# A chunk scan whose keys are turned by a product with a diagonal of decays, and whose state is advanced in PSUM

## The reference

```
def step(s, inp):
    r_t, w_t, k_t, v_t, kk_t, a_t = inp
    sa = einsum('bhvk,bhk->bhv', s, kk_t)
    s = s * w_t - sa (kk_t * a_t)^T + v_t k_t^T
    return s, einsum('bhvk,bhk->bhv', s, r_t)
```

## Time and profile before

| | us |
|---|---|
| three runs | 2038.17, 2038.21, 2041.07 |
| median | 2038.21 |
| profiled execution, its own time | 2040.22 |
| its span in the profile | 2038.6 |
| PE busy | 1709.5 (84%) |
| DVE busy | 1323.0 (65%) |
| ACT busy | 631.4 (31%) |
| POOL busy | 1162.7 (57%) |

### The profile page before, as it was taken

One profiled execution on the slowest core, in us unless ns is written; L12 is line 12 of the kernel. 1 busy time (PEld: TensorE's weight loads), 2 busy tenths in 40 slices (PEclk: granted clock), 3 DMA queues, 4 the chain that ended last, 5 costly groups with the idle time before them and its releaser, 6 DMA issues.

```text
span 2038.6 us, 25920 instructions
## 1 busy us (share of the span) xinstructions
PE 1709.5 (84%) x8602; PEld 827.1 (41%) x8602; DVE 1323.0 (65%) x3428; ACT 631.4 (31%) x1490; POOL 1162.7 (57%) x1555
## 2 busy tenths in 40 slices
PE   7999999889878999899989777777777777777776
PEld 2544435777765644444444222222222222222222
DVE  1278873577765886566666667666676666766653
ACT  3245532356543432322222222222222222222221
POOL 2100012565543767766667777776777776777773
PEclk9999999999999999999999999999999999999999
DMA  7356645445456999999999999999999999999996
GB/s 259 97 191 231 213 133 169 127 126 126 120 185 215 380 379 407 405 405 405 405 406 409 409 409 409 409 409 401 409 409 409 409 409 376 408 410 409 409 410 238
DMA packets 282158, 659.72 MB, mean 324 GB/s; under 512 B 71248, under 2 KB 120496, under 8 KB 282032
## 3 DMA queue, kind: packets, MB, share of 16 engines
q0 software_dynamic: 150336, 552.67, 68.4%
q1 hardware_dynamic: 131696, 105.46, 17.2%
HBM read 635.49 MB, written 22.54 MB: 323 GB/s over the span
## 4 chain that ended last, share of the span: by engine, by line
DMA 34%; PE 19%; POOL 9%; issue 4%; DVE 3%; ACT 1%; SPq 0%; POOLq 0%; ACTq 0%; DVEq 0%
DMA arena<-in_peer_v_dram,arena 28%; PE banks L2006 10%; POOL arena L1607 9%; DMA arena<-in_peer_u_dram,arena 5%; PE banks L2027 4%; PE banks L557 3%; DVE arena L1946 2%; PE banks L1508 1%; DMA arena<-in_w_out_dram 1%; PE banks L2077 0%; PE banks L2035 0%; POOL arena L1642 0%; DVE arena L1918 0%; PE banks L1516 0%; DVE arena L1844 0%
## 5 line engine op out<-in xcount | busy, mean ns | idle before, releaser
L2006 PE MATMUL banks<-arena 128*128 128x512 f32 x1984 | 948.6, 608 | 247.3 <-DMA arena<-in_peer_v_dram,arena 228.7
L1946 DVE CUSTOM_DVE_ANT_0 arena<-arena,banks 128x1024 f32<-128x1024 f32 x512 | 623.3, 1220 | 398.5 <-DMA arena<-in_peer_u_dram,arena 398.4
L2006 PEld LDWEIGHTS banks<-arena 128*128 128x128 f32 x1984 | 347.6, 190 | 836.3 <-issue 466.0
L1607 POOL DMA_INDIRECT arena<-in_peer_v_dram,arena x504 | 472.1, 937 | 218.1 <-PE banks L2006 114.3
L1607 POOL DMA_INDIRECT arena<-in_peer_u_dram,arena x512 | 481.8, 941 | 185.8 <-issue 130.5
L1660 ACT ACTIVATE arena<-arena 128x128 f32<-128x128 f32 x496 | 190.3, 400 | 695.3 <-PE banks L2006 694.5
L1135 PE MATMUL banks<-arena 64*64 64x64 f32 (+1 forms) x2688 | 109.1, 232 | 14.1 <-POOL arena L789 6.3
L2617 PE MATMUL banks<-arena 128*128 128x512 f32 x224 | 111.8, 606 | 0.7 <-ACT arena L2275 0.7
L1135 PEld LDWEIGHTS banks<-arena 64*64 64x64 f32 x2688 | 96.5, 138 | 29.0 <-issue 12.8
L2713 PE MATMUL banks<-arena 128*128 128x512 f32 x192 | 86.9, 609 | 1.2 <-issue 1.2
L2027 PE MATMUL banks<-arena 128*128 128x384 f32 x256 | 85.5, 485 | 0.8 <-ACT arena L1370 0.8
(11 more groups left out here) (325 smaller groups left out, 2023.3 us busy)
## 6 DMA issues: line engine op xcount, KB each, us to landing
arena<-in_w_mod_dram SPq DMA_DIRECT2D x18, 1024.0 KB, 7.2
arena<-in_peer_wq_dram SPq DMA_DIRECT2D x16, 1024.0 KB, 12.4
arena<-in_w_in_dram SPq DMA_DIRECT2D x27, 512.0 KB, 7.6
arena<-in_peer_u_dram,arena POOLq DMA_INDIRECT x512, 16.6
arena<-in_peer_v_dram,arena POOLq DMA_INDIRECT x512, 16.6
arena<-in_w_mod_dram SPq DMA_DIRECT2D x3, 2048.0 KB, 12.1
bk_scratch<-arena POOLq DMA_DIRECT2D x8, 768.0 KB, 3.6
kr_scratch<-arena POOLq DMA_DIRECT2D x8, 768.0 KB, 6.0
```

Source lines behind the costliest of these rows:

```text
L1607: pool.indirect_dma_start(ring[:, j % RING, :], None, table, bass.IndirectOffsetOnAxis(ap=idx[:, hi % 4, j:j + 1].bitcast(U32), axis=0)).t ...
L1946: nc.vector.tensor_tensor_reduce(u_ring[:, j % RING, :], u_ring[:, j % RING, :], h2cur, 1.0, 0.0, ALU.mult, ALU.add, acts[:, h % 2, j:j + ...
L2006: m = nc.tensor.matmul(PO[h][:, :], diag[:, j % 4], v_ring[:, j % RING, 512 * h:512 * h + 512], start=hp == 0 and j == 0, stop=hp == HEADS ...
```

## The change

The decay of a chunk moves from the end of the chunk to its keys and its old state. A diagonal matrix of the decays of each chunk is made on VectorE (`spread_decays`: one 128x512 product of the identity with the decays, and two 64x256 products that write the decays into the diagonal quarters of `IK`), for each direction of each block. The keys are turned by a matmul with that diagonal in place of a transpose, so that they come out turned and scaled. The old state through `IK` is no longer put into `C1`, but accumulated in `C2` onto the product with `RB`; `advance` is then two copies. GpSimd's identities, the tile `TMPS` and two semaphores go.

```
-    FV = {"ge": 1, "go": 2}
+    FV = {"ge": 1, "go": 2, "dg": 3}
...
-        identities(0)
-        identities(1)
...
-                    act.wait_ge(state_decayed, 11 * cp + 4 * cb + i + 1)
+                act.wait_ge(state_read_split, 4 * mm + i + 1)
...
-            nc.vector.tensor_tensor(TMPS, C1[:, 2 * P:3 * P].rearrange("p (d c) -> p d c", c=DH),
-                                    decay.unsqueeze(2).broadcast_to([P, 2, DH]), ALU.mult).then_inc(state_decayed, 1)
...
-            for d in range(2):
-                ...
-                for rows in (LOW, HIGH):
-                    last = nc.vector.scalar_tensor_tensor(dst[rows, rows], C2[rows, P * d + rows.start:P * d + rows.stop],
-                                                          pc_all[rows, 2 * cp + d, c:c + 1], TMPS[rows, d], ALU.mult, ALU.add)
+            at = [2 * (NB * d + ITEMS[d][ni]) for d in range(2)]
+            halves = SV[nb % 4].rearrange("p d (n c) -> p (d n) c", c=DH)
+            for h, rows in enumerate((LOW, HIGH)):
+                dst = halves[rows, at[0] + h:at[1] + h + 1:at[1] - at[0]]
+                src = C2[rows, 0:2 * P].rearrange("p (d c) -> p d c", c=P)[:, :, rows]
+                last = nc.vector.tensor_copy(dst, src)
             last.then_inc(state_written, 1)
+
+        def spread_decays(m, d):
+            p, b = m // 3, m % 3
+            first = NB * ORDER[d][b]
+            decay = pc_all[:, 2 * p + d, first:first + NB]
+            if m:
+                dve.wait_ge(front_products[d], NFP * (m - 1) + FP["bkT"])
+            if m >= 4:
+                dve.wait_ge(chunk_applied, 4 * (m - 3))
+            nc.vector.tensor_tensor(decay_diag[:, d], ident.unsqueeze(1).broadcast_to([P, NB, P]),
+                                    decay.unsqueeze(2).broadcast_to([P, NB, P]), ALU.mult)
+            for rows in (LOW, HIGH):
+                last = nc.vector.tensor_tensor(IK[m % 4][rows, d, :, rows], ident[rows, rows].unsqueeze(1).broadcast_to([DH, NB, DH]),
+                                               decay[rows].unsqueeze(2).broadcast_to([DH, NB, DH]), ALU.mult)
+            last.then_inc(front_vector[d], 1)
...  (in VectorE's do)
             corrections(m, 0)
+            if nxt is not None:
+                spread_decays(nxt, 0)
             split(chain, 1)
...
             split(chain, 3)
+            if nxt is not None:
+                spread_decays(nxt, 1)
             advance(chain, 3)
...  (before the loop, for blocks 0 and 1)
             odd_products(0, d)
+            spread_decays(0, d)
...  (read_state: the four matmuls with IK into C1 go; apply_chunk:)
-                for cols in (LOW, HIGH):
-                    m = nc.tensor.matmul(C2[cols, P * d:P * d + P], v3(QQ[mm % 2][:, d])[:, ITEMS[d][i], cols], RB[:, d],
-                                         start=True, stop=True)
+                ci = ITEMS[d][i]
+                inverse, state = v3(QQ[mm % 2][:, d])[:, ci], v3(SV[mm % 4][:, d])[:, ci]
+                for cols, other in ((LOW, HIGH), (HIGH, LOW)):
+                    m = nc.tensor.matmul(C2[cols, P * d + other.start:P * d + other.stop], inverse[:, cols], RB[:, d, other],
+                                         start=True, stop=True)
+                if (cb, i) == (2, 3):
+                    continue
+                for cols in (LOW, HIGH):
+                    nc.tensor.matmul(C2[cols, P * d + cols.start:P * d + cols.stop], inverse[:, cols], RB[:, d, cols],
+                                     start=True, stop=False)
+                for cols in (LOW, HIGH):
+                    m = nc.tensor.matmul(C2[cols, P * d + cols.start:P * d + cols.stop], IK[mm % 4][:, d, ci, cols], state[:, cols],
+                                         start=False, stop=True)
...  (turn_inputs)
-            four(lambda i: nc.tensor.transpose(W2[d][:, P * i:P * i + P], BKs[m % 2][:, d, i], ident), front_products[d])
+            pe.wait_ge(front_vector[d], NFV * m + FV["dg"])
+            four(lambda i: nc.tensor.matmul(W2[d][:, P * i:P * i + P], BKs[m % 2][:, d, i], decay_diag[:, d, i], start=True, stop=True),
+                 front_products[d])
```

More of the change, by code:

```diff
@@ L210, in _layer @@
     RB = cut(2, P)
-    TMPS = cut(2, DH)
     cut = Cut(PP_AT + NPP, MOD)
@@ L216, in _layer @@
     Yb = cut(NXC, 2, 2, DH)
+    decay_diag = cut(2, NB, P)
     LE, LO, SV, IK = [LE0, LE1, LE2, LE3], [LO0, LO1, LO2, LO3], [SV0, SV1, SV2, SV3], [IK0, IK1, IK2, IK3]
@@ L353, in _layer @@
     reads_loaded = [sem(f"reads_loaded{d}") for d in range(2)]
-    identities_placed = sem("identities_placed")
     front_products = [sem(f"front_products{d}") for d in range(2)]
@@ L368, in _layer @@
     state_read_split = sem("state_read_split")
-    state_decayed = sem("state_decayed")
     y_from_state = sem("y_from_state")
@@ L731, in pool4 @@
         pool.wait_ge(spilled_done, 16 * 5 * PAIRS)
-        placed = [0]
-        def identities(k):
-            for rows in (LOW, HIGH):
[L737 to L740, removed]
         S = slice(0, 8 * 2 * NB)
@@ L962, in advance @@
             dve.wait_ge(chunk_applied, 4 * mm + i + 1)
-            dve.wait_ge(state_decayed, 11 * cp + 4 * cb + i + 1)
-            for d in range(2):
-                c = NB * ORDER[d][cb] + ITEMS[d][i]
-                dst = v3(SV[nb % 4][:, d])[:, ITEMS[d][ni]]
-                if ni == 0:
-                    dve.wait_ge(front_scalar[d], NFS * nb + FS["v"])
-                for rows in (LOW, HIGH):
-                    last = nc.vector.scalar_tensor_tensor(dst[rows, rows], C2[rows, P * d + rows.start:P * d + rows.stop],
-                                                          pc_all[rows, 2 * cp + d, c:c + 1], TMPS[rows, d], ALU.mult, ALU.add)
-            last.then_inc(state_written, 1)
+            if ni == 0:
+                for d in range(2):
+                    dve.wait_ge(front_scalar[d], NFS * nb + FS["v"])
+            at = [2 * (NB * d + ITEMS[d][ni]) for d in range(2)]
[4 more added lines that the diff above has]
+                last = nc.vector.tensor_copy(dst, src)
+            last.then_inc(state_written, 1)
+        def spread_decays(m, d):
[12 more added lines that the diff above has]
+            last.then_inc(front_vector[d], 1)
         def even_products(m, d):
@@ L1062, in vector4 @@
             odd_products(1, d)
+            spread_decays(1, d)
         conv_rows(3)
@@ L1088, in read_state @@
                                              state[:, own], start=True, stop=True)
[L1089 to L1093, removed]
-                    for cols in (LOW, HIGH):
-                        m = nc.tensor.matmul(C1[cols, 2 * P + DH * d:2 * P + DH * d + DH], IK[mm % 4][:, d, ci, cols],
-                                             v3(SV[mm % 4][:, d])[:, ci, cols], start=True, stop=True)
             m.then_inc(state_read, 1)
```

6 lines of the change are left out of this document (removed).

## The result

The median went from 2038.21 us to 2048.32 us (five runs each), a ratio of 1.0046 [1.0034, 1.0058]: slower, by about 10 us where +0.3 was forecast, and beyond the range. (One of the five runs after, 2120.74 us at a mean clock of 0.846 against 0.99, is left out of the ratio.) The profiled execution took 2046.66 us, 6.4 more than that of before (spans 2045.1 and 2038.6).

What follows compares the result with a forecast made beforehand. A block was taken as TensorE's queue, stretched where VectorE comes late. Terms 1.7 + 0.4 - 0.8 - 0.5 + 1.8 - 0.3 - 2.0 = +0.3 us on 2038.21 gave 2038.5; own range 2034.5 to 2042, eight in ten 2032 to 2046.

Steps and rivals of the forecast that it cites:

- Block: 20.68, +0.2: A plain block, first read to first read, walked through TensorE's and VectorE's queues: 20.68 us after against 20.45 before.
- Ahead of apply 1: Plain block's start to apply 1: 7.55 us against 7.33, the earlier read offset by diagonals ahead of split 1; +0.22.
- From apply 1 on: Rest of a plain block, TensorE nearly dense: 13.13 us against 13.12, savings offset by longer applies and turns.
- the diagonals stand in front of split 1: Slower rival: diagonals beyond 1.2 us delay apply 1 in nine blocks; 2044 to 2046 us, chance 0.25.
- block 10 has no front and gains 1.4, ... net -0.3: Scan's end: block 10 gains 1.4 us, block 11 still waits for GpSimd's inverse; some -0.3 remains.
- Before the loop and block 0: Longer turns on TensorE delay block 1's triangles and GpSimd's inverse, +0.9, and block 0 itself, +0.8; together +1.7 us.
- Blocks 5 and 8: Blocks where TensorE waits for ScalarE behind the pair's moves: later pair turn and longer key turn, +0.9 us each.
- Tail: After the scan's blocks: read to read falls from 3.85 to about 3.2 us, last apply shorter; -2.0 in all.
- the turn by matmul at 0.98: TensorE's turn of keys: eight passes take 0.98 us in place of 0.49, +0.98 a block for two directions.
- read 1 earlier: Plain block: the read of chunk 1 comes at 3.74 us in place of 4.78, over a microsecond earlier.
- the chain is what counts: Faster rival: the chunk's chain, 0.65 us shorter, sets the time; 2023 at TensorE's bound, 2032 in between; chance 0.2.
- every 64x256 product in the rows has the same 0.42: VectorE's diagonals: argument, against a slowdown beside a busy GpSimd, that such products all take 0.42 us.

Runs made afterwards that it cites:

- no_diagonals: Changed kernel with a one-column VectorE copy in place of each diagonal from block 4's front on, so another output; 2037.96 us, ratio 0.9991.
- filled_wait: Changed kernel with five unread 512-column matmuls laid into TensorE's wait for GpSimd in block 11; 2049.62 us, ratio 1.0057.
- short_sum: Changed kernel with GpSimd's sum of pair 2 cut to an eighth, so another output; 2046.75 us, ratio 1.0041.
- idle_products: Kernel before, with the change's six products added at VectorE's block end, where nobody reads them; 2048.51 us, ratio 1.0049.
- after_again: The changed kernel run once more, unedited; 2049.69 us, ratio 1.0049 against the kernel before.
- clear_of_sums: Changed kernel, VectorE-scaled keys turned by transposes, products at VectorE's block end except those of blocks 6 and 9, left in place; 2034.0 us, 0.9978.

## Why the prediction was wrong

The sum's failed step is **"Block: 20.68, +0.2"**, the walk of a plain block. It stands, with an allowance for each kind of block, behind blocks 1 to 9, and each of them changed by 0.71 to 0.85 more than forecast (block 7 counted from block 4's 21.67); blocks 1 and 2 came out at 21.45 and 21.51, past the prediction's own mark of being wrong (over 0.5 from 20.45). The walk named the right mechanism, even the right wait, but its sizes were short:

- *Ahead of apply 1* it had 7.55 and the trace has 8.00. Of the 0.45, 0.28 are the diagonals (1.38 predicted, 1.66), 0.09 the read (0.51, then 0.61), 0.08 the copies (0.43, then 0.51). no_diagonals shows that this place pays one for one: 1.5 to 1.6 a block.
- *From apply 1 on* it had 13.13 and the trace has 13.51. The apply goes on for 0.85 (0.77 predicted), three times, and the reads for 0.61 where the next instruction is of another form. The rate of 0.51 was read before a matmul of the same shape (L1095 behind L1087), which the change removes; before anything else it goes on 0.1 longer (in block 2, 412.47 to 413.09). Against these 0.4, the forecast wait of 0.1 for split 3 did not come.
- *A slip in the same term:* the walk took its waits (0.95) from block 3, whose last read (434.68) has no old state behind it, and took off two old-state parts as for blocks 1 and 2. Block 2's waits there are 0.72. It did no harm, by luck: each wait is counted from the end of a row, some 0.07 behind the pace, which hides about 0.2 more of it.

In all 0.8 a block: nine blocks give 7.0 (with block 7 of before taken at block 4's 21.67). The range missed it because each term's error was allowed for alone (0.1 more a product, or an apply of 1.0), while the diagonals, the apply, the reads and the copies erred together in the same direction. The rival **"the diagonals stand in front of split 1"** was right in mechanism and place; it put 2044 to 2046 on diagonals of up to 2.0 or an apply of 1.0, and a smaller error of each, with the read's and the copies', gave as much in the blocks (0.3 and 7.0 more would be 2045.5). Blocks 10 and 11 and the clock account for what lies beyond.

The second failed step is **"block 10 has no front and gains 1.4, ... net -0.3"**: measured +2.2. Block 10 gained 1.0, but block 11's first products came 1.3 later, counted from block 10's start (21.38 before, 22.65 after), and the rest of block 11, at a clock of 0.92, took 0.9 longer. Of the 1.3, 1.2 is the inverse's later return from scratch. Of the clock, filled_wait's one profile says that it does not fall when the wait is filled, which is worth 1.1 us in the block; the time of the runs did not follow. Why the DMA lands later is open: it carries the same bytes and the same loads are queued behind it, and in short_sum it is not late. Every kernel with the new chain that keeps the sum in its place has 21.9 to 26.4 us in block 11 against 19.4 and 19.55. idle_products has 21.98 with the old chain and no later return, all by the clock. So a late return and a low clock add up here, and what makes each of them is not shown.

The other steps. *Before the loop and block 0*, +1.7, measured +1.1. *Blocks 5 and 8*: longer as foreseen, by the common 0.8 more. *Tail*: 3.2 from read to read predicted, 3.57 measured, for the same reason as the blocks (apply and read with other forms behind them). Two of the three stretches so gained 0.3 and not 0.6; the first went from 5.34 to 4.49, for before it held a wait of 0.58 for `w_out`. *Behind the tail*: 1.1 given back that the prediction did not have, and that is the clock of the output projection in this profile (0.80, then 1.00: 1.7), less 0.4 lost ahead of it: luck, as after_again does not have it. *Block 7*: it gains 1.5 that no step spoke of, since the granted clock is 1.00 after and 0.93 before, in both profiles of before. The terms together: 0.3 + 7.0 - 1.5 - 0.6 + 2.5 + 0.4 - 1.1 = 7.0, the shift seen at the routing. The medians lie 10 apart, the two profiled runs 6.4: the first profile after is the lowest of its five runs, and in after_again block 11 took 3.7 more, block 3 1.5 and the projection 1.7.

Right were: the turn by matmul at 0.98 (0.99) and the single pass of a transpose; read 1 earlier, by 0.8 where 1.0 was forecast; a wait of 1.5 for split 1 in its place (1.66); the second diagonals and ScalarE's and GpSimd's parts of a plain block off the path. The rival **"the chain is what counts"** holds for the kernel that could have been: with no diagonals in the way the blocks are 1.0 shorter, and 1.6 with the shorter turn too. Its bound of 18.8 was too low for the change as it stands, since TensorE's work grew by 1.0 and not by 0.4 (no_diagonals has 19.44); that clear_of_sums comes to 18.84, with another turn, is chance.

One argument of the prediction was unsound: "every 64x256 product in the rows has the same 0.42", against a cost beside GpSimd. Those products read one operand from PSUM; the added ones read both from SBUF. In the changed kernel this cost little on VectorE (1.60 to 1.66 for what takes 1.48 alone), more on GpSimd: block 3's inverse, in one stretch beside the diagonals:

```profile
429.93 0.73 DVE L953 TENSOR_TENSOR arena<-arena 128x512 f32<-128x512 f32 x1
430.59 0.91 DVE L956 TENSOR_TENSOR arena<-arena 64x256 f32<-64x256 f32 x2
```

```profile
429.39 0.73 POOL L749 TENSOR_TENSOR arena<-arena 64x36 f32<-64x36 f32 x1
430.20 0.58 POOL L751 TENSOR_TENSOR arena<-arena 64x36 f32<-64x36 f32 x1
...
436.74 0.24 POOL L749 TENSOR_TENSOR arena<-arena 64x36 f32<-64x36 f32 x1
```

The same step takes 0.24 where VectorE is not at it. From the spread to the end of the inverse GpSimd needs 14.1 in place of 13.1, which the blocks with a front cover.

## What to carry to other kernels

An instruction that frees no one should not stand ahead of one that TensorE waits for: here the order on VectorE, not the amount, cost 1.5 us a block. The change pays, by 0.2%, only once its extra products stand behind the chain and clear of GpSimd's sums, and the keys are turned by transposes again. A duration is taken with its operands' places and with what follows it: a product of two SBUF operands is another instruction than one with PSUM, and the read goes on 0.1 longer before a matmul of another form than before its like. Where nine blocks share a walk, the range has to take the terms' errors added up, times nine.

## What the runs showed of the hardware

- VectorE's products of two SBUF operands and GpSimd's hold each other up: 0.68 becomes 1.64 to 1.66 for 128x512, a pair of 64x256 0.85 becomes 1.65 to 2.94, GpSimd's sums 3.99 become 4.44 to 4.64, its small steps 0.24 become up to 0.73. The Trainium skill, "SBUF — State Buffer", section "Who interferes with whom", has this: a VectorE instruction with two SBUF inputs contends with a GpSimd instruction that reads SBUF. The Trainium skill, "SBUF — State Buffer", section Terms, says that the loser is blocked until the other is done. The trace agrees on who contends; it agrees only partly on full blocking, since the six products (2.96 alone) and GpSimd's two pieces (6.4 alone) are both done 7.9 us after 437.76, and one after the other would have been 9.4.
- TensorE's granted clock: after idle stretches of 2.81 and 4.26 us, matmuls ran at the lower level's pace (1.97 for 1.15, 1.12 for 0.69); with the second stretch filled by unread matmuls they did not. Block 11 stood at 0.72 to 0.93 in most kernels of the new chain and at 1.00 before. Its first 32 matmuls took 1.28 behind waits of 2.01 and 2.16 (the two profiles of before), 1.72 behind 2.19 (idle_products) and 1.98 behind 2.29 (short_sum). How long the low pace then lasts differs between executions of one kernel (block 11 is 22.57 and 26.25 in the two profiles of the changed kernel), and this is not explained.
- Two copies of 64x128 out of PSUM take 0.59, and the next VectorE instruction starts 0.51 after the first of them (405.86 to 406.37 in the changed kernel).
